# Splitting the value tile's weights in the attention, the key tile's ahead of the second chunk, and moving the key copy, in a fused layer step

## What is computed

```
def token_mixer(xn, pos, p, attend, recur):
    qa, ka, va, qb, fb, ib, ogb, ga, gb = split_in(xn @ p['w_in'])
    qa = rope(rmsnorm(qa.reshape(b, t, A_HEADS, 2, A_DH), p['q_norm_g']), pos)
    ka = rope(rmsnorm(ka.reshape(b, t, A_HEADS, 2, A_DH), p['k_norm_g']), pos)
    oa = attend(qa, ka, va, p['lam'])          # two softmaxes, the second subtracted with weight lam
    oa = rmsnorm(oa, p['subln_g']) * (1.0 - p['lam_init'])
    qh = jax.nn.silu(qb)
    f = lb + (1.0 - lb) * jax.nn.sigmoid(fb)
    ob, s_new = recur(qh, 1.0 - f, jnp.log(f), ib)   # gated linear recurrence, in chunks
    ob = rmsnorm(ob, p['hgrn_norm_g']) * jax.nn.silu(ogb)
    ...
```

## Time and profile before

| what | value |
|---|---|
| median of 3 runs | 2418.45 us (2413.58 to 2418.67) |
| the profiled execution | 2415.66 us |
| its span (first to last instruction) | 2413.9 us |
| mean granted clock of TensorE | 0.991 of full speed |
| PE / DVE / ACT / POOL busy | 96% / 67% / 41% / 33% of the span |
| one head, start of chunk 0 to start of chunk 0 | 134.4 to 137.3 us |

### The profile page before, as it was taken

The page is one execution under the profiler, slowest core; times in us unless marked ns, Lnnn a source line. Parts: engine busy times, 40 slices in busy tenths (PEclk is TensorE's granted clock), DMA queues, the critical chain, the costliest instruction groups (busy, mean ns, idle before and its releaser), DMA issues. The chain is left out here.

```text
span 2413.9 us, 46025 instructions
## 1 busy us (share of the span) xinstructions
PE 2315.9 (96%) x18425; PEld 2165.1 (90%) x18425; DVE 1610.7 (67%) x2711; ACT 994.4 (41%) x2071; POOL 798.7 (33%) x1020
## 2 busy tenths in 40 slices
PE   7899999999999999999999999999999999999999
PEld 5788888888888888888888899998999999999999
DVE  5568686767767686766688615417866676667668
ACT  6465555655555555655433402114222222222221
POOL 1034152514344152524344214441322322232222
PEclk9999999999999999999999999999999999999999
DMA  7203022121213022221499713111111111111112
GB/s 270 88 27 117 27 66 86 55 89 48 87 43 109 28 67 85 63 81 42 182 344 350 271 44 115 44 57 38 53 44 45 44 52 44 46 44 51 43 48 95
DMA packets 75631, 213.18 MB, mean 88 GB/s; under 512 B 15770, under 2 KB 24602, under 8 KB 75418
## 3 DMA queue, kind: packets, MB, share of 16 engines
q1 hardware_dynamic: 74266, 206.05, 25.4%
q10 hardware_dynamic: 1152, 4.19, 0.4%
HBM read 175.49 MB, written 26.26 MB: 84 GB/s over the span
## 5 line engine op out<-in xcount | busy, mean ns | idle before, releaser
L170 PE MATMUL h_G<-xn_hi,h_w_hi 128*128 128x344 f32 x1392 | 468.5, 337 | 8.5 <-ACT h_d_oraw L858 5.0
L170 PE MATMUL h_G<-xn_hi,h_w_lo 128*128 128x344 f32 x1392 | 445.8, 320 | 0.0
L170 PE MATMUL h_G<-xn_lo,h_w_hi 128*128 128x344 f32 x1392 | 445.4, 320 | 0.0
L2313 POOL TENSOR_TENSOR h_w_lo<-h_w_raw,h_w_hi 128x1024 fp32r<-128x1024 f32 x87 | 210.0, 2414 | 400.7 <-ACT h_w_hi L2077 384.8
L2250 PE MATMUL t_ps<-hn_hi,h_w_hi 128*128 128x344 f32 x1032 | 330.9, 321 | 0.0
L2250 PE MATMUL t_ps<-hn_lo,h_w_hi 128*128 128x344 f32 x1032 | 330.4, 320 | 0.0
L2250 PE MATMUL t_ps<-hn_hi,h_w_lo 128*128 128x344 f32 x1032 | 330.2, 320 | 0.0
L1120 POOL TENSOR_TENSOR h_w_lo<-h_w_raw,h_w_hi 128x1024 fp32r<-128x1024 f32 x58 | 146.1, 2519 | 490.4 <-ACT h_w_hi L738 413.3
L170 PEld LDWEIGHTS h_G<-xn_hi,h_w_hi 128*128 128x128 f32 x1392 | 264.2, 190 | 45.8 <-issue 16.9
L170 PEld LDWEIGHTS h_G<-xn_lo,h_w_hi 128*128 128x128 f32 x1392 | 262.9, 189 | 4.9 <-issue 0.9
L170 PEld LDWEIGHTS h_G<-xn_hi,h_w_lo 128*128 128x128 f32 x1392 | 262.5, 189 | 0.0
(11 more groups left out here) (369 smaller groups left out, 5526.2 us busy)
## 6 DMA issues: line engine op xcount, KB each, us to landing
h_w_raw<-in_w_in SPq DMA_DIRECT2D x72, 512.0 KB, 4.4
h_w_raw<-in_w_ffn SPq DMA_DIRECT2D x66, 512.0 KB, 3.6
...
```

The lines of the kernel that those rows point to most:

```text
L170: ins = eng.matmul(out, w[:, k * P:(k + 1) * P], x[:, k, columns], start=(k == 0 and n == 0), stop=(k == n_k - 1 and n == 2))
L2313: pool.tensor_tensor(wlo[buf(n)][:, :], raw[n % 2][:, :], whi[buf(n)][:, :].bitcast(F32), ALU.subtract).then_inc(w_lo.sem, 1)
```

## The change

It does five things in the stage of the heads.

- `SPLIT_AT`: the v tile (index 6) is split at piece 2, in block 2 of the attention, and no longer at piece 16 (chunk 3). The k tile (index 5) is split at `FILL_PIECE`, ahead of piece 12's reading on ACT and ahead of the decoding columns' copies on POOL, and no longer at piece 13 (chunk 0 on ACT; chunk 1 on POOL).
- The loads of weights take the order of the splits (`LOAD_ORDER`), with tables for the buffer of each tile (`RAW_OF`) and for its turn. All loads but that of the next head's first tile now stand ahead of the rotation's transfers in SP's queue, and that one stands behind the first of them. The store of the previous head's recurrence output stands one load earlier.
- ACT's `levels` is cut in three, `fine_levels`, `top_level` and `edge_levels`; the key copy now stands ahead of `edge_levels`, in chunk 0 ahead of `top_level` too.
- POOL's two `squares` move from before chunk 0 into chunks 2 and 4, behind the cosine's product.
- The waits follow: PE, ACT and POOL wait for a split by its place in the new order.

```diff
--- before.py
+++ after.py
@@ -485,7 +485,13 @@
 REC_PIECES = ([13], [14], [15], [16], [17], [18], [19], [20])
 SIGMOID = [n for n, (t, j) in enumerate(PIECES) if TILES[t] in ("f", "qh", "og")]
 ADA_AT = {13: 0, 15: 1, 17: 2, 19: 3}
-SPLIT_AT = {1: 1, 4: 2, 7: 3, 10: 4, 13: 5, 16: 6, 19: 7}
+SPLIT_AT = {1: 1, 2: 6, 4: 2, 7: 3, 10: 4, 12: 5, 19: 7}
+LOAD_ORDER = (6, 2, 3, 4, 5, NTL + 1, NTL)
+SPLIT_ORDER = (0, 1, 3, 4, 5, 6, 2, 7)
+RAW_OF = (0, 1, 1, 0, 1, 0, 0, 0, 1, 0)
+RAW_TURN = (0, 1, 2, 2, 3, 3, 1, 4)
+RAW_BEFORE = {6: 0, 2: 1, 3: 6, 4: 2, 5: 3, NTL + 1: 4, NTL: 5, NTL + 2: NTL}
+SQUARES_AT = (2, 4)
 
 
 def level_view(ap, lv):
@@ -668,29 +674,32 @@
                 sp.dma_start(flat(o["k"][bass.ds(h, 1)]), kT[:, :]).then_inc(kv_stored.sem, 16)
                 sp.wait_ge(piece_read.sem, piece_read.at(h, 0))
                 sp.dma_start(flat(o["v"][bass.ds(h, 1)]), vT[:, :]).then_inc(kv_stored.sem, 16)
-                for t in range(2, NTL + (3 if no_next(h) else 2)):
-
-                    behind, r = {NTL: (1, 0), NTL + 1: (3, 1), NTL + 2: (2, 0)}.get(t, (2, t % 2))
+                def load(t):
+                    last = SPLIT_ORDER[RAW_BEFORE[t]]
+                    sp.wait_ge(hi_done.sem, hi_done.at(h, last))
+                    sp.wait_ge(lo_done.sem, lo_done.at(h, last))
+                    r = RAW_OF[t]
+                    sp.dma_start(raw[r][:, :], flat(wt[bass.ds(weight(h, t), 1)])).then_inc(loaded[r].sem, 16)
+
+                for t in LOAD_ORDER:
                     if t == 3:
                         load_ada(h, 0, 0)
                         load_ada(h, 1, 0)
-                    if t == 5 and h:
+                    if t == 4 and h:
                         store_branch(h - 1, 2)
                         store_branch(h - 1, 3)
-                    if t == NTL - 1:
+                    if t == NTL:
                         turn_piece(h, 0)
-                        turn_piece(h, 1)
-                        load_ada(h, 2, 14)
-                    if t == NTL:
-                        turn_piece(h, 2)
-                        load_ada(h, 3, 16)
-                        turn_piece(h, 3)
-                    if t == NTL + 1:
-                        turn_piece(h, 4)
-                        turn_piece(h, 5)
-                    sp.wait_ge(hi_done.sem, hi_done.at(h, t - behind))
-                    sp.wait_ge(lo_done.sem, lo_done.at(h, t - behind))
-                    sp.dma_start(raw[r][:, :], flat(wt[bass.ds(weight(h, t), 1)])).then_inc(loaded[r].sem, 16)
+                    load(t)
+                turn_piece(h, 1)
+                load_ada(h, 2, 14)
+                turn_piece(h, 2)
+                turn_piece(h, 3)
+                load_ada(h, 3, 16)
+                turn_piece(h, 4)
+                turn_piece(h, 5)
+                if no_next(h):
+                    load(NTL + 2)
 
                 if no_next(h):
                     sp.wait_ge(rows_ready.sem, 1)
@@ -713,12 +722,8 @@
 
         def raw_loaded(eng, h, t):
 
-            if t == NTL:
-                eng.wait_ge(loaded[0].sem, loaded[0].at(h, 4))
-            elif t % 2 == 0:
-                eng.wait_ge(loaded[0].sem, loaded[0].at(h, t // 2))
-            else:
-                eng.wait_ge(loaded[1].sem, loaded[1].at(h, t // 2 + 1))
+            sig = loaded[RAW_OF[t]]
+            eng.wait_ge(sig.sem, sig.at(h, RAW_TURN[t]))
 
         def used_wait(eng, h, t):
 
@@ -828,16 +833,23 @@
                     t = SPLIT_AT[n]
                     raw_loaded(act, h, t)
                     used_wait(act, h, t)
-                    split(slot(t % NTL), 0 if t == NTL else t % 2)
-
-            def levels(h, k):
+                    split(slot(t % NTL), RAW_OF[t])
+
+            def fine_levels(h, k):
 
                 act.wait_ge(lv_diff.sem, lv_diff.at(h, k + 1))
                 act.wait_ge(lv_k.sem, lv_k.at(h, k))
+                act.activation(L[:, 1:FINE + 1, :], df[:, :, :], ACT.Exp, scale=-1.0)
+
+            def top_level(h, k):
+
                 at = k * P
-                act.activation(L[:, 1:FINE + 1, :], df[:, :, :], ACT.Exp, scale=-1.0)
                 act.activation(L[:, LEVELS - 1, 0:HALF], braw[:, at:at + HALF], ACT.Exp, scale=-1.0, bias=braw[:, at + HALF - 1:at + HALF])
                 act.activation(L[:, LEVELS - 1, HALF:P], braw[:, at + HALF:at + P], ACT.Exp, bias=neg_mid[:, k:k + 1])
+
+            def edge_levels(h, k):
+
+                at = k * P
                 act.activation(L[:, 0, :], braw[:, at:at + P], ACT.Exp, scale=-1.0, bias=braw[:, at + P - 1:at + P])
                 act.activation(L[:, LEVELS, :], braw[:, at:at + P], ACT.Exp).then_inc(lv_exp.sem, 1)
 
@@ -891,16 +903,25 @@
                 act.wait_ge(ib_turned.sem, ib_turned.at(h, 1))
                 act.activation(ibtok[:, :], Sf, ACT.Copy).then_inc(ib_tok.sem, 1)
                 act.wait_ge(ib_tok.sem, ib_tok.at(h, 1))
-                levels(h, 0)
+                fine_levels(h, 0)
+                top_level(h, 0)
+                edge_levels(h, 0)
+                split_next(h, FILL_PIECE)
                 piece(h, FILL_PIECE)
                 read_values(NB - 1)
                 sigmoid(h, len(SIGMOID) - 1)
 
                 for k in range(NB):
                     if k + 1 < NB:
-                        levels(h, k + 1)
+                        fine_levels(h, k + 1)
+                        if k:
+                            top_level(h, k + 1)
                     act.wait_ge(rec_done.sem, rec_done.at(h, k + 1))
                     act.activation(kht[:, :], kht_ps, ACT.Copy).then_inc(kht_ready.sem, 1)
+                    if k + 1 < NB:
+                        if k == 0:
+                            top_level(h, 1)
+                        edge_levels(h, k + 1)
                     if k < 6 and not no_next(h):
                         qk_norm(qk_summed.at(h, k + 1), k % 2)
                     if k == 1 and no_next(h):
@@ -959,8 +980,8 @@
             def piece(h, n):
                 t, j = PIECES[n]
                 if j == 0:
-                    pe.wait_ge(hi_done.sem, hi_done.at(h, t))
-                    pe.wait_ge(lo_done.sem, lo_done.at(h, t))
+                    pe.wait_ge(hi_done.sem, hi_done.at(h, SPLIT_ORDER[t]))
+                    pe.wait_ge(lo_done.sem, lo_done.at(h, SPLIT_ORDER[t]))
 
                 pe.wait_ge(piece_read.sem, piece_read.at(h, n - 1 if n else 0))
                 w = SLOT[t]
@@ -1129,9 +1150,9 @@
                 if n in SPLIT_AT:
                     t = SPLIT_AT[n]
                     raw_loaded(pool, h, t)
-                    pool.wait_ge(hi_done.sem, hi_done.at(h, t))
+                    pool.wait_ge(hi_done.sem, hi_done.at(h, SPLIT_ORDER[t]))
                     used_wait(pool, h, t)
-                    lo_of(slot(t % NTL), 0 if t == NTL else t % 2)
+                    lo_of(slot(t % NTL), RAW_OF[t])
 
             def kept(name, src, h):
                 return pool.tensor_copy(c["s_" + name][:, bass.ds(h, 1), :].rearrange("p o n -> p (o n)"), src[:, T:NT])
@@ -1179,16 +1200,13 @@
                     if i == 5:
                         differences(h, 0)
                 differences(h, 1)
+                split_next(h, FILL_PIECE)
                 pool.wait_ge(sig_used.sem, sig_used.at(h, 9))
                 pool.wait_ge(piece_read.sem, piece_read.at(h, 9))
                 for n, src in (("f", fc), ("kk", kk), ("qh", qh), ("ib", ib), ("og", og)):
                     ch(kept(n, src, h))
                 ch.sync()
                 pool.sem_inc(sample_rec.sem, 1)
-                pool.wait_ge(pv_read.sem, pv_read.at(h, NB))
-                pool.wait_ge(o_normed.sem, o_normed.at(h, 0))
-                squares(h, oraw, 0)
-                squares(h, oraw, 1)
                 for k in range(NB):
                     if k + 2 < NB:
                         differences(h, k + 2)
@@ -1196,6 +1214,10 @@
                         pool.wait_ge(piece_read.sem, piece_read.at(h, 12 + k + 1))
                         pool.wait_ge(qk_turned[k].sem, qk_turned[k].at(h, 4))
                         pool.tensor_tensor(rg[k % 2][:, :], rg[k % 2][:, :], cos[:, cols(k % NP)], ALU.mult).then_inc(qk_cos.sem, 1)
+                    if k in SQUARES_AT:
+                        pool.wait_ge(pv_read.sem, pv_read.at(h, NB))
+                        pool.wait_ge(o_normed.sem, o_normed.at(h, 0))
+                        squares(h, oraw, SQUARES_AT.index(k))
                     for n in REC_PIECES[k]:
                         split_next(h, n)
                 ch.reset()
```

## The result

Four runs of the changed kernel give a median of 2381.7 us (2379.65 to 2385.31), against 2418.56 (2413.58 to 2422.03) of the kernel before beside it: a ratio of 0.9847, interval 0.9835 to 0.9859, or 36.9 us less. The profiled execution has a span of 2380.5 us, 33.4 less than before. The forecast was 2389.5 us, 29.0 less.

The account below looks back on a forecast made before the run. PE, 96% busy, was the bound, its idle time lying in the recurrence's waits. Seven heads at 3.33 us (23.3), 1.1 in the last and 4.6 of clock give 29.0 us less: median 2389.5 us, range 2377 to 2402.

Parts of the forecast that it names:

- POOL's chain: From the key tile's `lo_of` through copies, differences and cosine: each us later from L1308 moves chunk 2's start one us.
- Chunk 0: The moved `lo_of` holds the last sigmoid product until 579.68; `operands` still ends earlier, 0.26 us won, 1.2 idle left.
- Chunk 1: Without `lo_of` the rotation's first product is not held; 2.36 us won up to chunk 2's start, 0.26 idle left.
- Chunks 2 to 5: Moved squares hold the rotation's first product: 0.13 us lost in chunk 3, 0.31 in chunk 5; chunk 4 wins 1.21.
- Chunk 6: The next head's `lo_of` stays; ACT and POOL are taken to be ahead, 0.2 us won of 0.31 idle.
- The attention: Block 2: v tile's split costs nothing; `lo_of` may hold L1276 some 0.6 us, covered by 2 us.
- The clock: Chunk 2 of three heads runs at clock 0.79 behind chunk 1's idle 2.4 us; 4.6 us go with that idle.
- The sum: 3.33 us a head, seven times 23.3, last head 1.1, clock 4.6: together 29.0 us.
- No hold: Rival: L1308 and the two L1220 run in 0.52 us in the new places; 2374 us, chance 0.07.
- DVE first: Rival: L1220 starts ahead of the squares, which wait instead; 0.63 us a head, 2385 us, within the forecast's 0.70.
- Less is won: Rival: `lo_of` holds `weigh` in the attention (2409), or chunk 0's idle lowers the clock (2394 or 2406); chance 0.19.
- slower: Rival: `lo_of` waits for the key tile's load, at 6 us later 2438 us; slower or nothing, chance 0.04.

Follow-up runs that it names:

- squares_back: Changed kernel with both of POOL's squares back ahead of chunk 0's differences: 2398.35 us.
- k_tile_only: Kernel before with only the k tile's split moved, on both engines: 2415.59 us, ratio 0.9982.
- key_back: Changed kernel with ScalarE's key copy behind all five exponentials again, as before: 2382.75 us.
- next_late: Changed kernel with POOL's split of the next head's first tile waiting for the operands of the last chunk: 2377.88 us.
- store_back: Changed kernel with the stores of the head before one place later in SyncE's load order, as before: 2382.49 us.

## Why the prediction was right, point by point

The forecast's mechanism held: the holds that go, the hold that comes in chunk 0, and POOL's chain that decides P2. It failed in chunk 6, and it had no term for the attention. It forecast 29.0 us; the profile has 37.7 in the heads. Behind the heads 4.6 are lost and ahead of them 0.25 won, which leaves the span's 33.4; these two parts change by as much between kernels that leave them alone. The measured 2381.7 us lies inside the range (2377 to 2402), at the edge of the forecast's own bounds (2382 to 2397), and not for the reasons given for that edge: the squares' delay and the hold in chunk 6 are both there, and what came on top are the attention and heads longer than the fourth.

*Chunk 0.* L1330 was forecast from 577.61 to 579.68, 3.39 us behind P0. It ended at 561.38 + 2.10 = 563.48, or 3.42. The win is 0.47 us against 0.26, as P1 − P0 is 7.21 us where 7.42 was worked out: `assemble` starts 0.08 earlier, and it and `operands` take 3.76 instead of 3.88. The wait left is 0.96 where 1.2 stood.

*Chunk 1.* P2 was forecast 2.36 earlier with chunk 0's part, and is 2.59. The wait left is 0.40, forecast 0.26. It was this step that rested on POOL's chain, and squares_back and k_tile_only show the chain directly: put back or left there, the squares keep chunk 1 at 8.15 to 8.17 us with L1242 unheld.

*Chunks 2 to 5.* The two holds of L1242 in chunks 3 and 5 are there, 1.34 us each. But of the forecast idle of 0.32 us at P4 only some 0.1 came (6.37 us with 6.27 of PE's work), and P4 is at P2 + 12.78, forecast 13.01. DVE's chain does set P4, as the step had it; each of its terms was a little too long. L1242 ends at P2 + 7.56 (forecast 7.69, from 0.6 us of delay by the key copy, which was 0.5), then 1.27 us to L1356 (1.32), 3.83 to the end of L1348 (3.88), and 0.12. Squares_back gives the price of the squares' hold by itself: 0.18 a chunk (6.37 against 6.19). Chunk 3 won 0.08 where 0.13 should be lost, and chunk 5 lost 0.17 where 0.31 should be. Chunk 4 won 1.31, forecast 1.21. By key_back the key copy's move is what pays for the squares there, as the prediction said.

*Chunk 6.* Here 0.2 us should be won, and 0.07 were lost. The step that failed is "since P6 is itself waited for, ACT and POOL are ahead by then, and I take 0.2 won". With the key copy where it was, it comes true: in key_back chunk 6 lasts 7.68 us, 0.24 less than the 7.92 of before. What the step left out is the key copy's own effect on ACT's split in this chunk, which comes 0.35 us later, and `lo_of` with it. The prediction had such a delay, but only for the differences of chunk 2. It also overlooked that `lo_of` holds DVE's product here already before (2.16 us in eight heads), so that the end of `lo_of` sets P7. Fixing the order in next_late takes hold and wait away.

*The attention.* The sum has no term for it, and 0.29 us were won in the fourth head, 3.4 in seven. The store's place was in the diff, and the prediction gave it no price; store_back shows 0.29 a head for it, and the 1.4 us beyond that are for the most part the fifth head's longer wait for the same store. The v tile's split cost nothing there, as forecast. The hold that it could bring came: L1298 (L1276 before) takes 0.62 us in block 2 of each head and not 0.17, and ends with `lo_of`. ACT reads its result only 1.1 us or more behind its end, which covers the hold, and store_back's attention is as long as that of before without the fifth head (83.23 and 83.21). The pair in the fourth head of the changed kernel, DVE and POOL (`lo_of` ends at 501.88, L1298 at 501.91):

```profile
501.29 0.62 DVE L1298 TENSOR_SCALAR h_d_sm<-h_d_sm 128x2 f32<-128x2 f32 x1
```

```profile
499.36 2.52 POOL L1141 TENSOR_TENSOR h_w_lo<-h_w_raw,h_w_hi 128x1024 fp32r<-128x1024 f32 x1 [5.22 <-issue]
```

*The clock.* Its 4.6 us are gone. In the seven kernels in which PE is idle for 0.34 to 0.63 us in chunk 1, no chunk 2 is slow, in 49 of 49 heads; in the five with 1.7 to 2.4 us it is slow in 17 of 35. Chunk 0's idle goes from 0 to 1.2 us in the first and from 0 to 1.8 in the second.

*The sum again.* In the fourth head the parts differ from the forecast's 3.33 by 0.23, 0.23, 0.10, 0.14, −0.27 and 0.29: 4.05. Seven times 0.72 is 5.0. The forecast took seven heads like the fourth, but the fourth was the shortest of before, while two of after (129.87 and 130.00) are well below its 130.36: 2.9 more, the clock's 4.6 us not counted. The last head won 1.83 where 1.1 was taken. Together 8.7, which is 37.7 − 29.0.

*The rivals.* "No hold" is refuted by L1330 and L1242. "DVE first" was a rival for the squares, and did not come there; it came in heads 1, 5 and 8 at chunk 6. "Less is won", by a lower clock or the attention, did not come. Nor did "slower" come: the split started 0.27 behind the differences, so its load was there.
